# A two-layer encoder trunk in fp32 by three products: up projections and the last down projection with tokens as weights, VectorE squares and transfers within SBUF, attention's result taken from PSUM

## The chip, the cores and the metric

The kernel runs on one core of a Trainium2 chip. The metric is the device time of one execution in microseconds; the time before is 2311.02 us, the median of three runs (2310.91 to 2311.66). The profiled execution took 2311.02 us as well, of which its span in the profile is 2309.3 us; 1.7 us lie around the span.

## The reference, cut to what matters

One sequence of 256 tokens with 2048 features goes through two layers, all in fp32. Layer 0 is attention (16 heads with a relative-position bias over a band of chunks, 16 query heads with a sliding window of two chunks and sinks, rotary), layer 1 a gated linear recurrence. Each is followed by cross-attention into 256 memory tokens (4 heads of 128) and by a gated feed-forward with a causal depthwise convolution over time:

```python
def conv_ffn(h, w_up, conv_w, conv_b, w_down):
    u = causal_depthwise_conv(h @ w_up, conv_w, conv_b)     # h (256, 2048), w_up (2048, 11264), width 3
    val, gate = jnp.split(u, 2, axis=-1)
    return (jax.nn.gelu(gate) * val) @ w_down               # w_down (5632, 2048)
x = x + conv_ffn(rms_norm(x, ffn_norm[layer]), ffn_w_up[layer], ...)
```

The convolution mixes tokens t, t-1 and t-2 of one feature, with weights that belong to the feature.

## The kernel before, in words

**Arithmetic.** Each operand x is split in x_hi (x rounded to fp32r, the type that TensorE multiplies at full rate) and x_lo = x - x_hi, and a product is w_hi x_hi + w_hi x_lo + w_lo x_hi, summed in PSUM. Activations live feature-major: features on the 128 partitions, 256 tokens along the free dimension (`xT`, 16 tiles of 128 features). `xg_hl` and `a_hl` hold the hi and lo halves of a stage's input.

**Units.** All weights come as one stream of 788 units of 128 x 1024 fp32 (512 KB), through four slots. SP loads unit c into `raw` (line 466) once VectorE has split the unit four before it (`lo_done`). ScalarE rounds it to `w_hi` (`split_hi`, line 320) once TensorE has finished the unit four before it (`pe_unit`). VectorE forms `w_lo` (`split_lo`, line 326). TensorE multiplies. The order on every engine is written out by hand as a program per engine; semaphore counts tie the programs together, so an instruction that waits holds everything behind it on its engine.

**Two forms of a unit.** `pair_unit` (lines 342 to 363) has the weights stationary and the tokens moving: 4 feature tiles x 2 output tiles x (one matmul of 512 columns, w_hi against hi and lo side by side, and one of 256 columns, w_lo against hi). The result stands feature-major in two banks, in two halves (main and cross part), which VectorE adds later. `token_unit` (lines 379 to 400) has the tokens stationary and the weights moving: 2 feature tiles x 2 token tiles x three matmuls of 512 columns; the result stands token-major in two banks. Before the change, the attention's input projection and the projections of the memory use the token form, the other large products the pair form; cross-attention has its own two (lines 338 and 374).

**Stages.** In order: `tok` (input projection), `mem` (memory projections, between the attention's groups), `out0`, `xq0`, `xo0` (cross-attention), `up0`, `down0`, `rec`, `out1`, `xq1`, `xo1`, `up1`, `down1`. An up stage has 176 units: the first 8 are woven between units of the cross-attention's output (`WOVEN`), the rest is a loop of 11 iterations of 16 units, one iteration giving 4 value tiles and 4 gate tiles. A down stage has 88 units.

**The feed-forward before.** When a block of 4 units is complete, ScalarE copies its cross part (line 1210), VectorE adds main and cross part into `u_buf` (line 1694) and multiplies by the norm factor per token (line 1653), which TensorE has broadcast over the partitions once per stage (`bcast_pe`, line 439). Then ScalarE makes the tap of the present token with the bias (line 1173), VectorE adds the two earlier tokens' taps (lines 1660, 1665), ScalarE does the GELU (line 1157), VectorE the product (line 1680), ScalarE its rounding (line 1168), VectorE the rest (line 1684). `UP_STEPS` says in which slot of the 16 each step stands.

**Attention before.** Eight groups of four heads. Per group: scores on TensorE (lines 627, 633), softmax on VectorE and ScalarE, 12 transposes (line 650), a copy of these to SBUF, two banks by ScalarE (line 1015) and one by VectorE (line 1454), values (line 665), copy to `oT` (line 1472). Memory units lie between. After the last group ScalarE rounds `oT` (line 1046) and VectorE forms the rest (line 1478), and `out0` starts as the tiles come.

**The end before.** `down1` adds each block to `xT` in two VectorE steps (lines 1537, 1538) and SP writes each pair of tiles (line 507).

Of the kernel before, what the change touches and what calls it, by code (L numbers as in the profile page):

```python
# [16 lines left out]
P = 128  # L17
D_MODEL, SEQ, N_MEM = 2048, 256, 256
KT = D_MODEL // P
# [14 lines left out]
NEG = -1e30  # L34

# [14 lines left out]
WOVEN = [("x", 0), ("x", 1), ("x", 2), ("x", 3), ("x", 4), ("u", 0), ("x", 5), ("x", 6), ("u", 4), ("x", 7), ("u", 1), ("u", 5),  # L50
         ("u", 2), ("u", 6), ("u", 3), ("u", 7)]
UP_STEPS = {0: {8: "g0", 11: "v0", 14: "g1"},
            1: {2: "last", 5: "g0", 8: "v0", 11: "g1", 15: "v1"},
            None: {3: "g0", 7: "v0", 11: "g1", 15: "v1"}}
# [5 lines left out]
UP_BANK = (4, 6, 0, 2)  # L60
# [28 lines left out]
def trunk(nc, t):  # L89
# [3 lines left out]
    with ctx:  # L93
# [19 lines left out]

        xT = sb("xT", [KT, SEQ])
# [8 lines left out]
        a_hi, a_lo = a_hl[:, :, 0, :], a_hl[:, :, 1, :]  # L123
        R1 = AR + size([KT, 2, SEQ])
        R2 = R1 + size([FT - KT, SEQ])
        FFN = top[0]
        u_buf = sb("u_buf", [4, SEQ + 2])
        y_buf = sb("y_buf", [4, SEQ])
        kmem = [at("kmem0", FFN, [XA_HEADS, N_MEM]), sb("kmem1", [XA_HEADS, N_MEM])]
        vmem = [at("vmem0", FFN + 4096, [TT, XA_W]), sb("vmem1", [TT, XA_W])]  # L130
        kmem_tok = [at("kmem_tok0", FFN, [TT, XA_W]), at("kmem_tok1", FFN + size([4, SEQ + 2]) + size([4, SEQ]), [TT, XA_W])]
# [35 lines left out]
        oT = at("oT", O0, [KT, SEQ])  # L167
# [11 lines left out]
        bias_at = [at("bias0", FFN + size([4, SEQ + 2]) + size([4, SEQ]), [3 * COLS]), at("bias1", XG + 12288 + 6144, [3 * COLS])]  # L179
# [10 lines left out]
        x_sq = {name: y_buf if name == "down0" else at(f"x_sq_{name}", R2 + 20480, [4, SEQ])  # L190
# [12 lines left out]
        gate_w = at("gate_w", R2 + 12288, [2, 4, P])  # L203
        cross = at("cross", AR + size([FT - 1, 2, SEQ]), [2, SEQ])
# [27 lines left out]
        pT_ps, pT_act, pT_dve, o_ps, o_done = sem("pT_ps"), sem("pT_act"), sem("pT_dve"), sem("o_ps"), sem("o_done")  # L232
        oT_hi, oT_lo = sem("oT_hi"), sem("oT_lo")
# [7 lines left out]
        tap_done, conv_done, gelu_done = sem("tap_done"), sem("conv_done"), sem("gelu_done")  # L241
# [9 lines left out]
        sp_exp, sp_done = sem("sp_exp"), sem("sp_done")  # L251
        out_done = sem("out_done")
# [15 lines left out]
        for name, k in (("out0", N_BLOCKS), ("xo0", N_BLOCKS), ("up0", FT), ("down0", N_BLOCKS), ("rec", 16), ("out1", N_BLOCKS),  # L268
                        ("xo1", N_BLOCKS), ("up1", FT), ("down1", N_BLOCKS)):
            fblock[name] = n  # L270
            n += k

        cblock = {"up0": 0, "rec": FT, "up1": FT + 16}
# [105 lines left out]
        def token_unit(pe, c, k0, nk, hi, lo, bank, start, stop, ready=None):  # L379

            s, n = c % SLOTS, UE // nk
            if c == 0:
                pe.wait_ge(hi_half, 1)
            else:
                pe.wait_ge(hi_done, c + 1)
            for k in range(nk):
# [4 lines left out]
                for tt in range(TT):  # L391
                    for q, a in enumerate((hi, lo)):
                        nc.tensor.matmul(ps[:, bank + tt, 0:n], a[:, k0 + k, tt * P:tt * P + P], w_hi[:, s, k * n:k * n + n],  # L393
                                         start=start and k == 0 and q == 0, stop=False)
            pe.wait_ge(lo_done, c + 1)
# [6 lines left out]


# [17 lines left out]
        BC = [FFN0, REC, FFN1]  # L421
# [14 lines left out]
        def bcast_pe(pe, n):  # L436
            pe.wait_ge(rb_ready, BC.index(n) + 1)
            for tt in range(TT):
                last = nc.tensor.matmul(ps[:, 2 if n in (FFN0, FFN1) else 6, tt * P:(tt + 1) * P], rb[:, tt, :], ident[:, :],
                                        start=True, stop=True)  # L440
            last.then_inc(rbc_ps, 1)

        def bcast_act(act, n):
            act.wait_ge(rbc_ps, BC.index(n) + 1)
            nc.scalar.activation(r_bc[:, :], ps[:, 2 if n in (FFN0, FFN1) else 6, 0:SEQ], ACT.Copy).then_inc(rbc_ready, 1)

        def sum_squares(pool, src, tiles):

            ch = chains["pool"]
            for tile in tiles:  # L450
# [7 lines left out]
                  (mask[:, :], "mask"), (sinks[:, :, :], "sinks"), (rconst[:, :, :], "rconst"), (fconv[:, :], "fconv0")]  # L458

# [4 lines left out]
        def _(sp):  # L464
# [34 lines left out]
            with sp.Fori(4, N_UNITS // SLOTS) as i:  # L499
                for s in range(SLOTS):  # L500

                    sp.wait_ge(lo_done, i * SLOTS + (s + 1 - SLOTS))
                    unit(s, i * SLOTS + s)
            for b in range(N_BLOCKS):

                sp.wait_ge(proj_free, fblock["down1"] + b + 3)
                sp.dma_start(t["out_t"][:, 2 * b:2 * b + 2, :], xT[:, 2 * b:2 * b + 2, :]).then_inc(out_done, 16)
            sp.wait_ge(out_done, 16 * N_BLOCKS)
# [11 lines left out]
        def pair_tiles(buf, first_tile, n, i=None, per=0):  # L520

            if i is None:
                return buf[:, first_tile:first_tile + n, :]
            return buf[:, bass.ds(i * per + first_tile, n), :]

        def column(buf, index, i=None, per=0):

            return buf[:, index:index + 1] if i is None else buf[:, bass.ds(i * per + index, 1)]
# [5 lines left out]
        SQ_BEFORE = {"out0": 0, "xo0": N_BLOCKS, "down0": 2 * N_BLOCKS, "out1": 3 * N_BLOCKS, "xo1": 4 * N_BLOCKS}  # L534

        AFTER = {"out0": XA0, "xo0": FFN0, "down0": REC, "out1": XA1, "xo1": FFN1, "down1": None}
        UNITS = {"out0": U_BLOCK, "out1": U_BLOCK, "xo0": U_XA_OUT, "xo1": U_XA_OUT, "down0": U_DOWN, "down1": U_DOWN}

        UP_DVE, GATES_AT = 12, 4
        LAST_STEPS = {0: (8,), 1: (9, 10), 2: (11,), 3: (12,), 4: (13,)}  # L540

        def block_done(name, b0, pos):
# [4 lines left out]
            return pos // UNITS[name] if pos % UNITS[name] == UNITS[name] - 1 else None  # L547

# [6 lines left out]
        def _(pe):  # L555
# [42 lines left out]
            def mem_unit(f):  # L598
# [5 lines left out]
                elif u == 0:  # L604

                    pe.wait_ge(mem_free, b)
# [1429 lines left out]
```

## Time and profile before

| | |
|---|---|
| runs | 2311.66, 2311.02, 2310.91 us |
| profiled execution | 2311.02 us, span 2309.3 us, granted clock 1.00 |
| busy | TensorE 2299.1 us (100%), VectorE 1574.2 (68%), ScalarE 1256.0 (54%), GpSimd 189.8 (8%) |
| DMA | 426.94 MB, 185 GB/s on average |

A row of the view of groups gives line, engine, operation, output<-inputs, shapes and count, then the busy time, the mean of one in ns, and the idle time before it with what ended it. A row of the timeline gives start, length, engine, line, operation and count; matmuls are pipelined, so the time of a group of them is read from start to start.

### The profile page before, as it was taken

To read this page: it belongs to the slowest core of one execution; us is meant where nothing else is said; L and a number is where in the kernel's file an instruction comes from. 1 tells how busy PE (TensorE), PEld (TensorE's weight loads), DVE (VectorE), ACT (ScalarE), POOL (GpSimd) and SP (SyncE) were. 2 spreads that over 40 slices of the span, in tenths; PEclk is the share of its full clock that TensorE was granted. 3 is DMA by queue.
4 is the path that set the end of the run, shared out by engine and by line. 5 is a ranking of instruction groups with operands and counts; after the bars stand their busy time and mean duration, and the time that the engine had idled before them with its cause. 6 is when DMAs were issued, how large, how long until landed. Compare 5 with 4: busy or idle time off the path is not lost.

```text
span 2309.3 us, 38203 instructions
## 1 busy us (share of the span) xinstructions
PE 2299.1 (100%) x13184; PEld 2005.1 (87%) x13184; DVE 1574.2 (68%) x1963; ACT 1256.0 (54%) x1701; POOL 189.8 (8%) x171
## 2 busy tenths in 40 slices
PE   9999999999999999999999999999999999999999
PEld 7888888998888888888888888898888888888888
DVE  6776776577777777755555778668777777774443
ACT  6645564466555555544444776556555555553332
POOL 1710002130000000000000100222000000000000
PEclk9999999999999999999999999999999999999999
DMA  8656335445555555555555555535555555555554
GB/s 278 206 189 205 134 117 182 164 164 185 179 200 188 185 190 184 196 190 189 191 187 188 178 184 185 197 133 195 185 191 187 178 200 189 184 190 191 191 187 158
DMA packets 118942, 426.94 MB, mean 185 GB/s; under 512 B 13600, under 2 KB 14496, under 8 KB 118864
## 3 DMA queue, kind: packets, MB, share of 16 engines
q1 hardware_dynamic: 116928, 418.31, 52.9%
q0 software_dynamic: 1792, 7.52, 0.9%
q8 instruction: 51, 0.84, 0.2%
q14 instruction: 27, 0.22, 0.0%
q10 hardware_dynamic: 144, 0.06, 0.0%
HBM read 423.73 MB, written 2.10 MB: 184 GB/s over the span
## 4 chain that ended last, share of the span: by engine, by line
PE 98%; DVE 1%; ACT 1%; issue 0%; DMA 0%; SPq 0%; ACTq 0%; DVEq 0%
PE ps L353 53%; PE ps L357 26%; PE ps L393 8%; PE ps L398 4%; PE ps L338 2%; PE ps L374 2%; PE ps L665 1%; PE ps L852 1%; PE ps L650 0%; PE ps L735 0%; PE ps L572 0%; PE ps L756 0%; DMA xT<-in_x_t 0%; PE ps L633 0%; PE ps L627 0%
## 5 line engine op out<-in xcount | busy, mean ns | idle before, releaser
L326 DVE TENSOR_TENSOR w_lo<-raw,w_hi 128x1024 fp32r<-128x1024 f32 x788 | 970.2, 1237 | 539.5 <-ACT w_hi L320 537.0
L320 ACT ACTIVATE w_hi<-raw 128x1024 fp32r<-128x1024 f32 x787 | 827.3, 1056 | 635.9 <-PE ps L357 499.8
L353 PE MATMUL ps<-xg_hl,w_hi 128*128 128x512 f32 x3328 | 1046.4, 396 | 0.0
L357 PEld LDWEIGHTS ps<-xg_hl,w_lo 128*128 128x128 f32 x3328 | 625.2, 188 | 147.8
L357 PE MATMUL ps<-xg_hl,w_lo 128*128 128x256 f32 x3328 | 653.8, 278 | 0.0
L353 PE MATMUL ps<-a_hl,w_hi 128*128 128x512 f32 x1920 | 603.1, 395 | 0.6 <-DVE a_hl L1478 0.6
L353 PEld LDWEIGHTS ps<-xg_hl,w_hi 128*128 128x128 f32 x3328 | 506.9, 189 | 0.2
L357 PEld LDWEIGHTS ps<-a_hl,w_lo 128*128 128x128 f32 x1920 | 360.7, 188 | 85.2
L357 PE MATMUL ps<-a_hl,w_lo 128*128 128x256 f32 x1920 | 377.2, 278 | 0.0
L353 PEld LDWEIGHTS ps<-a_hl,w_hi 128*128 128x128 f32 x1920 | 292.3, 189 | 0.7 <-DVE w_lo L326 0.7
L1210 ACT ACTIVATE cross<-ps 128x512 f32<-128x512 f32 x104 | 62.0, 596 | 144.5 <-PE ps L357 144.5
L393 PE MATMUL ps<-w_hi,xg_hl 128*128 128x512 f32 (+1 forms) x576 | 136.2, 379 | 1.2 <-DVE xg_hl L1295 1.2
L1173 ACT ACTIVATE y_buf<-u_buf,fconv 128x256 f32<-128x256 f32 x176 | 96.2, 594 | 53.2 <-DVE u_buf L1653 53.2
L393 PEld LDWEIGHTS ps<-w_hi,xg_hl 128*128 128x128 f32 x576 | 103.2, 188 | 21.4 <-DVE xg_hl L1295 1.1
L1694 DVE TENSOR_TENSOR u_buf<-cross,ps 128x512 f32<-128x512 f32 x84 | 57.7, 687 | 89.3 <-ACT cross L1210 89.3
L1660 DVE SCALAR_TENSOR_TENSOR y_buf<-u_buf,fconv,y_buf 128x256 f32<-128x256 f32 x176 | 77.9, 479 | 0.0
L1665 DVE SCALAR_TENSOR_TENSOR y_buf<-u_buf,fconv,y_buf 128x256 f32<-128x256 f32 x176 | 76.9, 478 | 0.1
L398 PE MATMUL ps<-w_lo,xg_hl 128*128 128x512 f32 (+1 forms) x288 | 73.1, 378 | 0.0
L1168 ACT ACTIVATE a_hl<-y_buf 128x512 f32 (+1 forms) x44 | 27.8, 632 | 79.5 <-DVE y_buf L1680 79.5
L393 PE MATMUL ps<-w_hi,a_hl 128*128 128x512 f32 x256 | 66.0, 400 | 0.9 <-ACT kmem_tok L982 0.6
L1653 DVE TENSOR_TENSOR u_buf<-u_buf,r_bc 128x512 f32<-128x512 f32 x88 | 60.8, 691 | 2.6
L398 PEld LDWEIGHTS ps<-w_lo,xg_hl 128*128 128x128 f32 x288 | 52.1, 188 | 10.4 <-DVE w_lo L326 0.4
(198 smaller groups left out, 1486.4 us busy)
## 6 DMA issues: line engine op xcount, KB each, us to landing
raw<-in_w_stream SPq DMA_DIRECT2D x787, 512.0 KB, 3.3
bias<-in_rel_bias POOLq DMA_DIRECT2D x4, 768.0 KB, 6.3
memT<-in_mem_t POOLq DMA_DIRECT2D x4, 512.0 KB, 6.5
gate_w<-in_gate_w POOLq DMA_DIRECT2D x4, 512.0 KB, 3.7
out_t<-xT SPq DMA_DIRECT2D x8, 256.0 KB, 4.3
xT<-in_x_t SPq DMA_DIRECT2D x2, 512.0 KB, 7.6
xT<-in_x_t SPq DMA_DIRECT2D x3, 256.0 KB, 8.9
raw<-in_w_stream SPq DMA_DIRECT2D x2, 256.0 KB, 4.0
```

Source lines behind the costliest of these rows:

```text
L320: nc.scalar.activation(w_hi[:, s, :], raw[:, s, :], ACT.Copy).then_inc(hi_done, 1)
L326: nc.vector.tensor_tensor(w_lo[:, s, :], raw[:, s, :], w_hi[:, s, :].bitcast(F), ALU.subtract).then_inc(lo_done, 1)
L353: nc.tensor.matmul(ps[:, bank + m, :], w_hi[:, s, w], both, start=start and k == ks[0], stop=False, skip_group_check=True)
L357: last = nc.tensor.matmul(ps[:, bank + m, SEQ:2 * SEQ], w_lo[:, s, w], x[:, xk, 0, :], start=False, stop=stop and k == ks[-1], skip_group_ ...
L393: nc.tensor.matmul(ps[:, bank + tt, 0:n], a[:, k0 + k, tt * P:tt * P + P], w_hi[:, s, k * n:k * n + n], start=start and k == 0 and q == 0, ...
L398: last = nc.tensor.matmul(ps[:, bank + tt, 0:n], hi[:, k0 + k, tt * P:tt * P + P], w_lo[:, s, k * n:k * n + n], start=False, stop=stop and ...
L1173: A(y_buf[:, m, :], u_buf[:, m, 2:2 + SEQ], ACT.Identity, scale=column(fconv, w + 2, i, 32), bias=column(fconv, w + 3, i, 32)).then_inc(ta ...
L1210: A(cross[:, :, :], ps[:, bank:bank + 2, SEQ:2 * SEQ], ACT.Copy).then_inc(cross_ready, 1)
L1653: V.tensor_tensor(part, part, r_bc[:, :].unsqueeze(1).to_broadcast([P, 2, SEQ]), ALU.mult).then_inc(u_scaled, 1)
L1660: middle.append(ch.mark(V.scalar_tensor_tensor(y_buf[:, m, :], u_buf[:, m, 1:1 + SEQ], column(fconv, 4 * (4 * half + m) + 1, i, 32), y_buf ...
L1665: ins = V.scalar_tensor_tensor(y_buf[:, m, :], u_buf[:, m, 0:SEQ], column(fconv, 4 * (4 * half + m), i, 32), y_buf[:, m, :], ALU.mult, ALU ...
L1694: V.tensor_tensor(u_buf[:, tile:tile + 2, 2:2 + SEQ], cross[:, :, :], ps[:, bank:bank + 2, 0:SEQ], ALU.add).then_inc(proj_free, 1)
```

## The change

**Up stages.** The units use the token form: 8 units of 512 columns are half an iteration, first the gate half, then the value half, in banks 4, 5 and 6, 7. ScalarE evacuates both banks into `y_up` with the token's norm factor as scale. The columns are ordered on the host so that VectorE can turn 32x32 squares (`up_turn`, into `z_t`) and SP can move the squares to their partitions with 16 transfers within SBUF (`moves`, into `u_t`): for this, token 2q + t stands at place 128t + q of the norm's output (`by_tile_order`), and a run of 64 tokens of each feature lies in `u_t` behind a halo of four places, of which GpSimd copies the two that are needed. `y_up` lies in the memory of `u_t`, so ScalarE waits for `conv_done` before it evacuates. Taps and convolution run half an iteration behind, in slots 12 and 13 for the gate half and 4 and 5 of the next iteration for the value half; product in slot 6, rounding in 7, rest in 8. The last iteration's value half is done in the first slots of the down stage.

**Last down.** Token form, 4 blocks of 22 units. `xT` is turned and moved to `x_tok` (token-major) by four VectorE turns and 16 transfers in `up1`. SP writes token-major output.

**Attention.** The result goes straight from PSUM to hi and lo; the transposed probabilities are all copied by ScalarE; groups 4 to 7 leave out the first 64 keys for the later 128 queries; memory banks are released one by one.

```diff
-WOVEN = [("x", 0), ("x", 1), ("x", 2), ("x", 3), ("x", 4), ("u", 0), ("x", 5), ("x", 6), ("u", 4), ("x", 7), ("u", 1), ("u", 5),
-         ("u", 2), ("u", 6), ("u", 3), ("u", 7)]
+WOVEN = [("x", 0), ("x", 1), ("x", 2), ("x", 3), ("x", 4), ("u", 0), ("x", 5), ("u", 1), ("x", 6), ("u", 2), ("x", 7), ("u", 3),
+         ("u", 4), ("u", 5), ("u", 6), ("u", 7)]
+        y_up = at("y_up", UT, [TT, COLS])
...
# SP, up stage
+                def moves(i, half, bs):
+                    sp.wait_ge(zt_ready, times(TT * (2 * l * UP_ITER + half + 1), i, 2 * TT))
+                    for b in bs:
+                        for a in range(4):
+                            sp.dma_start(u_t[SQ * b:SQ * b + SQ, a, :, :].rearrange("p k n -> p (k n)"),
+                                         z_t[SQ * a:SQ * a + SQ, b, :, :].rearrange("p k n -> p (k n)")).then_inc(ut_in, 16)
...
+                        if u in (7, 15):
+                            moves(i, u // 8, (0, 1))
+                        if u == 8:
+                            moves(i, 0, (2, 3))
+                        if u == 0 and i is not None:
+                            moves(i, -1, (2, 3))
...
# TensorE, up stage
-                        pair_unit(pe, c0 + u, k, xg_hl, 2 * (q % 2), k == 0, k == KT - 4, i, 4 * U_BLOCK)
+                        for u in range(8):
+                            token_unit(pe, c0 + 8 * half + u, 2 * u, 2, xg_hi, xg_lo, UP_BANK[half], u == 0, u == 7, None, None, i, U_UP)
-                bcast_pe(pe, (FFN0, FFN1)[l])
...
# ScalarE
+            def up_tiles(l, i, half):
+                b = 2 * l * UP_ITER + half
+                act.wait_ge(pe_unit, times(first[f"up{l}"] + 8 * (half + 1), i, U_UP))
+                if i is not None or b:
+                    act.wait_ge(conv_done, times(4 * b, i, 8))
+                for tt in range(TT):
+                    A(y_up[:, tt, :], ps[:, UP_BANK[half] + tt, :], ACT.Copy, scale=r_tok[:, (FFN0, FFN1)[l], tt:tt + 1]).then_inc(up_out, 1)
...
+                    for u in range(8 if i is None else 0, U_UP):
+                        split_hi(act, c0 + u + SLOTS, i, U_UP)
+                        if u < 9 and i is not None:
+                            value_slot(l, i, u)
+                        if u % 8 == 7:
+                            up_tiles(l, i, u // 8)
+                        if u in (12, 13):
+                            taps(l, i, 0, 0, (2 * u - 24, 2 * u - 23))
+                        if u == 14:
+                            gate_gelu(l, i)
...
# VectorE
+            def up_turn(l, i, half):
+                b = 2 * l * UP_ITER + half
+                if i is not None or b:
+                    dve.wait_ge(ut_in, times(MOVES * b, i, 2 * MOVES))
+                for tt in range(TT):
+                    dve.wait_ge(up_out, times(TT * b + tt + 1, i, 2 * TT))
+                    V.transpose(z_t[:, :, :, HALO:RUN].rearrange("p b k (i t) -> p t (b k) i", t=TT)[:, tt, :, :],
+                                y_up[:, tt, :].rearrange("p (c j) -> p c j", j=SQ)).then_inc(zt_ready, 1)
...
+            def value_slot(l, i, u):
+                if u in (4, 5):
+                    conv(l, i, 1, 1, (2 * u - 8, 2 * u - 7))
+                if u == 6:
+                    product(l, i, 1)
+                if u == 8:
+                    value_lo(l, i, 1)
...
# attention: ScalarE and VectorE
-                A(probsT[:, 0:2 * COLS], flat(ps[:, 3:5, :]), ACT.Copy).then_inc(pT_act, 1)
+                A(probsT[:, :], flat(ps[:, 3:6, :]), ACT.Copy).then_inc(pT_act, 1)
+                for e in range(2):
+                    A(out_part(g, e, 0), out_ps(e), ACT.Copy).then_inc(o_hi, 1)
-                    last = V.tensor_copy(flat(oT[part, 2 * g:2 * g + 2, :]), ps[part, 4 + e, :])
+                    last = V.tensor_tensor(out_part(g, e, 1), out_ps(e), out_part(g, e, 0).bitcast(F), ALU.subtract)
...
# last down: TensorE and VectorE
-            out_section("down1", g_lo, 2, FT // 2)
+                    for u in range(TOK_DOWN - (n == 3)):
+                        token_unit(pe, c0 + TOK_DOWN * n + u, 2 * u, 2, a_hi, a_lo, bank, u == 0, u == TOK_DOWN - 1,
+                                   value_there if n == 0 else None)
+                for tt in range(TT):
+                    dve.wait_ge(tile_ps, tt + 1)
+                    x = x_tok[:, 3, tt, :]
+                    V.tensor_tensor(x, x, ps[:, 2 + tt, :], ALU.add).then_inc(tile_done, 1)
```

## Rows read from the trace of the kernel before

**Rows 1.** The page's chain that ended last, by engine, share of the span.

```profile
PE 98%; DVE 1%; ACT 1%; issue 0%; DMA 0%; SPq 0%; ACTq 0%; DVEq 0%
```

**Rows 2.** Stretches: length, busy us (instructions) per engine, granted clock, DMA share, GB/s.

```profile
200.00:345.00 145.00, 142.72 (x768) 119.70 (x767) 112.71 (x159) 85.39 (x198) 6.87 (x12) 1.00 0.41 140
496.00:970.00 474.00, 473.98 (x2725) 413.48 (x2724) 356.24 (x472) 269.27 (x344) 4.43 (x5) 1.00 0.55 188
2047.00:2306.00 259.00, 258.46 (x1485) 225.32 (x1483) 126.64 (x119) 98.93 (x98) 0.00 (x0) 1.00 0.54 185
```

**Rows 3.** Timeline (start us, us) of ScalarE, up loop: GELU rows one iteration apart.

```profile
641.54 0.64 ACT L1157 ACTIVATE y_buf<-y_buf 128x512 f32<-128x512 f32 x1 [0.52 <-DVE y_buf L1665]
...
686.12 0.64 ACT L1157 ACTIVATE y_buf<-y_buf 128x512 f32<-128x512 f32 x1 [0.52 <-DVE y_buf L1665]
```

**Rows 4.** Timeline of TensorE, first projections in token form: unit starts, five units apart.

```profile
155.73 1.98 PE L393 MATMUL ps<-w_hi,xg_hl 128*128 128x512 f32 x8
...
169.33 1.98 PE L393 MATMUL ps<-w_hi,xg_hl 128*128 128x512 f32 x8
```

**Rows 5.** Timeline of TensorE, first down stage: sixteen steps apart.

```profile
1000.06 0.62 PE L353 MATMUL ps<-a_hl,w_hi 128*128 128x512 f32 x2
...
1011.20 0.63 PE L353 MATMUL ps<-a_hl,w_hi 128*128 128x512 f32 x2
```

**Rows 6.** Waits of TensorE: us in total, times, longest us.

```profile
PE ps L665 <- DVE probsT L1454: 0.8, 1, 0.8
PE ps L393 <- ACT kmem_tok L982: 0.6, 2, 0.3
PE ps L353 <- DVE a_hl L1478: 0.6, 1, 0.6
...
PE ps L393 <- ACT vmem L982: 0.3, 1, 0.3
```

**Rows 7.** Timeline of TensorE, attention, scores of one group.

```profile
267.06 1.13 PE L627 MATMUL ps<-bkT,bqT 64*128 64x256 f32 x8
268.04 0.60 PE L633 MATMUL ps<-bkT,bqT 64*128 64x128 f32 x4
```

**Rows 8.** Timeline of TensorE, first up stage, broadcast of the norm factors.

```profile
513.23 0.71 PE L439 MATMUL ps<-ident,rb 128*128 128x128 f32 x4
513.70 0.71 PE L353 MATMUL ps<-xg_hl,w_hi 128*128 128x512 f32 x2
```

**Rows 9.** Groups by line: count | busy us, mean ns of one | idle before.

```profile
L326 DVE TENSOR_TENSOR w_lo<-raw,w_hi 128x1024 fp32r<-128x1024 f32 x788 | 970.2, 1237 | 539.5 <-ACT w_hi L320 537.0
L1694 DVE TENSOR_TENSOR u_buf<-cross,ps 128x512 f32<-128x512 f32 x84 | 57.7, 687 | 89.3 <-ACT cross L1210 89.3
...
L320 ACT ACTIVATE w_hi<-raw 128x1024 fp32r<-128x1024 f32 x787 | 827.3, 1056 | 635.9 <-PE ps L357 499.8
L1210 ACT ACTIVATE cross<-ps 128x512 f32<-128x512 f32 x104 | 62.0, 596 | 144.5 <-PE ps L357 144.5
```

**Rows 10.** Timeline of GpSimd and VectorE, up stage: smallest row, two convolution passes.

```profile
506.97 0.71 POOL L425 TENSOR_TENSOR r_tok<-v_tok,neg_half 128x2 f32<-128x2 f32 x1 [3.80 <-DVE v_tok L418]
...
963.03 0.88 DVE L1660 SCALAR_TENSOR_TENSOR y_buf<-u_buf,fconv,y_buf 128x256 f32<-128x256 f32 x2
```

**Rows 11.** Timeline of SP's queue: first and last of five issues in a row.

```profile
34.50 0.43 SPq L475 DMA_DIRECT2D y_rot<-in_rope_g  x1
...
36.40 0.43 SPq L475 DMA_DIRECT2D fconv<-in_fconv  x1
```

**Rows 12.** The page's DMA issues: count, KB each, us to landing.

```profile
raw<-in_w_stream SPq DMA_DIRECT2D x787, 512.0 KB, 3.3
...
out_t<-xT SPq DMA_DIRECT2D x8, 256.0 KB, 4.3
```

**Rows 13.** Timeline at the end: the second of the last two additions, last output.

```profile
2306.22 0.69 DVE L1538 TENSOR_TENSOR xT<-xT,ps 128x512 f32<-128x512 f32 x1
2306.94 0.33 SPq L507 DMA_DIRECT2D out_t<-xT  x1
```

More of the change, by code:

```diff
@@ L498, in _, with units @@
             tables(TABLES)
[L499 to L508, printed above, removed]
+            def units(c0, c1):
+                with sp.Fori(c0 // SLOTS, c1 // SLOTS) as i:
+                    for s in range(SLOTS):
+                        sp.wait_ge(lo_done, i * SLOTS + (s + 1 - SLOTS))
+                        unit(s, i * SLOTS + s)
@@ L626, in scores @@
                     if tile:
-                        last = nc.tensor.matmul(ps[:, j % 2, col * SEQ:(col + 1) * SEQ], q[part, ft, P:SEQ], k, start=True, stop=True)
+                        near = 0 if g < 4 else CHUNK
+                        last = nc.tensor.matmul(ps[:, j % 2, col * SEQ + near:(col + 1) * SEQ], q[part, ft, P:SEQ], k[:, near:SEQ],
+                                                start=True, stop=True)
                     else:
@@ new lines, in conv @@
+            def conv(l, i, back, half, tiles):
+                b = 2 * (l * UP_ITER - back) + half
+                if tiles[0] == 0:
+                    dve.wait_ge(halo_done, times(b + 1, i, 2))
+                for j, count in ((1, mid_done), (0, conv_done)):
+                    for m in tiles:
+                        dve.wait_ge(tap_done if j else mid_done, times(4 * b + m + 1, i, 8))
+                        y = chunks(y_tile(half, m - 4 * back, i))
+                        V.scalar_tensor_tensor(y, u_t[:, :, m, HALO - 2 + j:RUN - 2 + j], column(fconv, 4 * (4 * (1 - half) + m) - 32 * back + j, i, 32),
+                                               y, ALU.mult, ALU.add).then_inc(count, 1)
@@ L1903, in cross_attention, with halos, halo @@
                     G.tensor_tensor(xs[:, 2, h, :], xs[:, 1, h, :], neg_half[:, 0:TT], ALU.pow).then_inc(xrq_ready, 1)
+            def halos(l):
+                def halo(i, half):
+                    pool.wait_ge(ut_in, times(MOVES * (2 * l * UP_ITER + half + 1), i, 2 * MOVES))
+                    one = ones[:, 0:24].rearrange("p (a k n) -> p a k n", a=3, k=4)
+                    G.tensor_tensor(u_t[:, 1:4, :, HALO - 2:HALO], u_t[:, 0:3, :, RUN - 2:RUN], one, ALU.mult).then_inc(halo_done, 1)
+                with pool.Fori(0, UP_ITER) as i:
+                    for half in range(2):
+                        halo(i, half)
             def gate_load(i):
@@ L1932, in _ @@
             out_section("xo1")
+            halos(1)
 def _stream(inp):
```

503 lines of the change are left out of this document (279 added, 224 removed).

## The prediction

> **What bounds the kernel now.** I read the page first, down to its chain of waits: 98% of the chain that ends last is TensorE [rows 1], so only what shortens TensorE's instruction stream, or one of its few waits, can gain. Next the view by stretches [rows 2]: in the up stage TensorE lacks 0.02 of 474 us of being always busy (the second up stage is alike), in the last down stage 0.5 us at its very end; only the attention stage has 2.3 us of idle time in 145. The granted clock is 1.00 in all of them. In the up stage VectorE works 356 us, ScalarE 269, the DMA engines 55%: cover, not bound. Last the pace, since nothing else counts. One weight tile of 128x1024 is a unit. In feature form (weights stationary) it is 16 matmuls, 8 of 512 columns and 8 of 256. In the up loop an iteration of 16 units takes 686.12 - 641.54 = 44.58 us [rows 3], 2.786 us per unit. In token form (tokens stationary) it is 12 matmuls of 512 columns; in the first projections five such units take 169.33 - 155.73 = 13.60 us [rows 4], 2.720 each. Both stream 6144 columns; the difference is four instructions. That it isn't the loop's edge is seen within the first down stage: 16 steps of four matmuls take 1011.20 - 1000.06 = 11.14 us [rows 5], 2.785 per unit, with no edge between.
>
> **The change part by part.**
>
> *Matmul form.* All 2 x 176 up units (8 of each layer are woven into the cross-attention output) and the 88 of the last down go from 16 to 12 matmuls. 440 x (2.786 - 2.720) = 29.0 us. Rows 4 are straight-line code while the up stages loop; since the edge of the old loop cost at most 44.58 - 16 x 2.785 = 0.02 us, I keep it, and let the term go from 25 to 31.
>
> Here a rule of the Trainium skill speaks against the change. Its page "TensorE: Matmul & The Clock Gate" gives the gap of back-to-back matmuls as N/2.4 ns plus about 2.5 ns. By it four fewer save 10 ns a unit, an estimate of 4.4 us in all. The rows have 66 ns a unit, 16 ns for each matmul dropped, and the trace does not agree with so small an overhead. I take the rows.
>
> *Attention.* ScalarE now takes the rounded half of its result from PSUM and VectorE the rest, with no copy that is split once all groups are done. At the start of the output projection TensorE waited 0.6 us for that (a_hl, line 1478); the first unit now needs only groups long done, the last group is asked for in the fourth. ScalarE copies all of the transposed probabilities, so the 0.8 us for VectorE's part (line 1454) goes; ScalarE's copy grows by a half and stays beside the 2.7 us unit that follows the transposes. Each memory bank is released by itself: the 0.6 and 0.3 us for kmem_tok and vmem go [rows 6]. Groups 4 to 7 score 192 keys, not 256: 8 records per group at (268.04 - 267.06)/8 = 0.122 us [rows 7], of which a quarter of the streaming goes, 64/2.4 = 27 ns; x 32 = 0.9 us. Together 3.2. What is late next is the next group's probabilities, two units or more ahead. Bounds 1 to 3.5.
>
> *Norm factors.* The factor per token becomes the scale of ScalarE's evacuation, so the broadcast over partitions goes in both up stages: on TensorE 513.70 - 513.23 = 0.47 us each [rows 8], 0.9 in all. VectorE loses four scalings and four sums of halves per iteration, 0.69 us each.
>
> *The new road of an up tile.* Per half iteration (8 units, 512 columns): ScalarE evacuates two banks (2 x 0.60), VectorE turns 2 x 128x512 in squares, SP issues 16 transfers of 32 rows x 1088 bytes, GpSimd fills the halos; then taps, convolution and product as before, in slots 4 to 8 and 12, 13. TensorE itself waits for banks freed eight units ago and for weights split three units ahead, so all this is hidden while it keeps pace.
> A turn is not in the trace. Below, it could cost ScalarE's 0.60 for 128x512; above, at half the rate, the 1.23 of a pass of 1024 columns [rows 9]. I take the 0.69 of VectorE's own pass of that shape. VectorE then has 16 x 1.23 + 16 x 0.44 + 2 x 1.23 + 4 x 0.69 = 32 of 43.5 us per iteration; ScalarE, 269/474 of it now [rows 2], does about as much as before.
> The page "VectorE: DVE Perf Modes" of the Trainium skill, section "The three transpose paths", gives 311 ns for 128x128 bf16 in 32x32 squares; four of those would be an estimate of 1.24 us, at my upper end, and no row here shows a turn.
> SP issues any size 0.475 us apart (four intervals, 34.50 to 36.40) [rows 11]: 16 moves + 8 loads are 11.4 of 21.8 us. The loads behind the moves go out up to 4 us late. A load is due some 3 units, 8 us, after its slot is free and lands in 3.3 [rows 12]: just covered, and its split is again 3 units ahead of TensorE. The moves add 0.56 MB to each 4.2 MB; 55% becomes 65 to 70%.
>
> *The circle.* The evacuated tile lies where the turned one does, so ScalarE first waits for the convolution of the half before: a chain that closes once per half. From the last landing, value half: halo 0.7 (GpSimd's 0.71), four passes of convolution 1.76 (0.88 for two) [rows 10], split 1.23, 1.76, split 1.23, product 1.23, rounding 1.05, evacuation 1.20, last turn 0.69: 10.9; 16 intervals of SP 7.6; landing 2.4 (the last output, issued 2306.94, ends the span of 2309.3 [rows 13]) to 3.3. Value 20.9 to 21.8. Gate: GELU 1.2 and a split on ScalarE 1.05 in place of split, product and rounding: 19.6 to 20.5. Both halves 40.5 to 42.3 us, TensorE's 16 units 43.5. It fits by 1.2 to 3.0, so I cost it at nothing; if longer, each microsecond costs 22 (11 iterations, 2 layers).
>
> *First down stage, an added wait.* The last value tiles are now finished in its first block, the rest in slot 8. VectorE has five splits, eight convolution passes, product and rest in slots 4 to 8, 12.2 us of 13.9, after a split that can't begin before the ninth unit's end: 1.05 + 1.23 + 1.23 = 3.5, with hand-overs 3.7 us behind it, where the eleventh unit asks 2.8 behind it. 0.9 us of wait; behind it on TensorE stands everything. Bounds 0 to 3. In the last down a block is 22 units, and the tiles are in time.
>
> *Residual in token form.* Four turns and 16 transfers of 128 KB in the last up stage, once; within the same cover. 0, bounds 0 to 4. At the end one addition is left after the last matmul where two stood, the second from 2306.22 [rows 13]: 0.7 us.
>
> *Sum.* 29.0 + 3.2 + 0.9 + 0.7 - 0.9 = 32.9 us. The profiled run's own time is 2311.02 us (span 2309.3, 1.7 around it), and the median of the runs is the same. 2311.0 - 32.9 = 2278.
>
> **The rivals.**
> *A: the circle is longer than 43.5 us.* For it: 1.2 to 3.0 us of slack, and neither a turn nor a transfer within SBUF has a row. With turns at 1.23 a half grows by 1.2 (two in a row), the iteration to 42.9 to 44.7; with landings of 4.3, as the outputs' [rows 12], to 44.3. One of the two costs up to 1.2 x 22 = 26 us: 2290 to 2304. Both make 40.5 + 2.4 + 3.8 = 46.7 us: 3.2 x 22 = 70, so 2348, slower than before. It turns at 43.5 + 32.9/22 = 45.0 us per iteration. Its place: ScalarE's evacuation waits for the convolution, the splits behind it are late, TensorE waits for w_lo. Against both: a move is a fifteenth of a load.
> *B: the form gives next to nothing.* By the rule of the skill's page 4.4 us of the main term are left, then 4.4 + 3.9 = 8 us and 2303. As a mechanism of this kernel it would mean that token units pay elsewhere in a loop what they save, 2.77 us each. Rows 5 speak against it.
> *C: late loads.* If the burst of 16 moves holds a load past its cover, TensorE waits in each half: 44 x 0.3 = 13 us, 2291. For it 11.4 us of issues in 21.8; against it 3 units of cover twice over.
>
> **How the numbers follow.** Forecast 0.75, A with one value bad 0.07, A with both 0.08, B 0.03, C 0.07. Predicted 2278 us. The range of 8 in 10 takes in the bounds of the terms (25 to 31, 1 to 3.5, waits up to 7), C and most of A's first case: 2272 to 2300. A measurement here tells 0.2%, 4.6 us, from no change. Faster 0.88, same 0.03, slower 0.09.
>
> **What would show it.** GELU rows 43.5 us apart in the up loops and TensorE without idle there: the main term. Turn rows near 0.69, moves landing in 2.4 to 3.3 us, an evacuation that waits for TensorE and not for VectorE: the circle. An idle of 1 us before the eleventh unit of the first down stage, none at the start of the attention's output. I am wrong if GELU rows stand more than 43.7 us apart.

## The result, and the profile after

| | us | lowest to highest |
|---|---|---|
| before, 4 runs | 2310.97 | 2310.86 to 2311.66 |
| after, 4 runs | 2366.76 | 2364.79 to 2370.56 |

The changed kernel is slower: ratio 1.0243, 95% interval 1.0231 to 1.0255, that is 55.8 us more where 33 less were forecast. The profiled execution took 2364.79 us, its span is 2363.0 us and its granted clock 0.996.

The page's chain and issues after, answering to [rows 1, 12]. An issue row gives count, KB each and the median us from issue to landing:

```profile
PE 58%; SPq 16%; DMA 8%; issue 6%; DVE 5%; ACT 5%; ACTq 1%; DVEq 0%
PE ps L408 18%; PE ps L366 16%; SPq L539 15%; PE ps L413 9%; PE ps L370 8%; DMA raw<-in_w_stream 8%; PE ps L351 2%; PE ps L387 2%; DVE y_iter L1785 2%; ACT w_hi L333 2%; ACT y_up L1287 1%; DVE z_t L1772 1%; ACT y_iter L1295 1%; SPq L491 1%; DVE w_lo L339 1%
...
raw<-in_w_stream SPq DMA_DIRECT2D x787, 512.0 KB, 3.5
u_t<-z_t SPq DMA_DIRECT2D x704, 34.0 KB, 1.9
```

TensorE had 98% of the chain and has 58%. SP's queue, at 0% before, has 16%, nearly all of it in line 539, the issue of the transfers within SBUF. Note that the transfers themselves (DMA u_t<-z_t) are not among the listed lines at all: it is the issuing that lies on the chain.

The stretches after (us, then busy us and instructions of TensorE, weight loads, VectorE, ScalarE, GpSimd, then clock, DMA share, GB/s), answering to [rows 2]:

```profile
500.00:1008.00 508.00, 482.63 (x2096) 391.06 (x2096) 324.97 (x407) 265.75 (x324) 9.22 (x25) 1.00 0.61 202
1600.00:2120.00 520.00, 493.17 (x2151) 399.41 (x2150) 336.61 (x421) 271.07 (x333) 15.66 (x29) 1.00 0.62 204
2120.00:2359.00 239.00, 235.69 (x1034) 194.62 (x1033) 115.65 (x107) 94.54 (x94) 0.24 (x1) 0.99 0.58 193
```

Both up stages lose: 25.4 and 26.8 us of idle TensorE, at full clock. No other engine is full and the DMA engines are at 61%. Idle time isn't all of the loss: for the same 11416 matmuls TensorE is busy 2291.7 us here and 2268.3 us in e1 below, a kernel that doesn't lose, so some 23 us lie in longer busy rows (the ends of matmuls are modelled). The pace shows both parts. ScalarE's GELU rows, one iteration apart, answering to [rows 3]:

```profile
722.80 1.06 ACT L1301 ACTIVATE y_iter<-y_iter  x1 [1.04 <-DVE y_iter L1785]
769.75 1.06 ACT L1301 ACTIVATE y_iter<-y_iter  x1 [1.04 <-DVE y_iter L1785]
...
958.92 1.06 ACT L1301 ACTIVATE y_iter<-y_iter  x1 [1.04 <-DVE y_iter L1785]
```

From 722.80 to 958.92 there are five iterations, 47.2 us each. Ten iterations take 471.9 us in the first up stage (534.30 to 1006.21) and 476.3 in the second, where the first of the ten takes 50.3 and the others 47.3. The form alone would give 435 for ten. So an iteration is 3.9 us too long on average, and 22 x 3.9 = 86 us is nearly all that separates the result from the forecast (2366.8 - 2278 = 89). SP's queue over one iteration, answering to [rows 11] (a row: start, length of the run of issues, count):

```profile
704.61 4.95 SPq L539 DMA_DIRECT2D u_t<-z_t  x8
709.76 0.43 SPq L491 DMA_DIRECT2D raw<-in_w_stream  x1
710.23 4.94 SPq L539 DMA_DIRECT2D u_t<-z_t  x8
715.37 11.21 SPq L491 DMA_DIRECT2D raw<-in_w_stream  x7
727.32 4.96 SPq L539 DMA_DIRECT2D u_t<-z_t  x8
...
751.51 4.95 SPq L539 DMA_DIRECT2D u_t<-z_t  x8
```

Eight issues take 4.95 us, 0.63 from one to the next with the last issue's own 0.5 at the end. The sixteen of a half, with the one load between them, hold SP from 704.61 to 715.2, where the prediction had 7.6 us. From the first of a half to the first of the next it is 22.7 us (727.32 - 704.61) for the gate half and 24.2 (751.51 - 727.32) for the value half; TensorE's eight units would take 21.8.

### The profile page after: what moved, and what is told of

The parts are those of the page before. It is cut to its first block, busy times and chain, and to the rows that moved or that the text cites. A ratio compares the mean times of both kernels' runs of the same rounds, so it can differ in the third digit from the quotient of the medians.

```text
span 2363.0 us, 34265 instructions
## 1 busy us (share of the span) xinstructions
PE 2291.7 (97%) x11416; PEld 1925.3 (81%) x11416; DVE 1494.1 (63%) x1808; ACT 1253.1 (53%) x1663; POOL 203.4 (9%) x215
## 4 chain that ended last, share of the span: by engine, by line
PE 58%; SPq 16%; DMA 8%; issue 6%; DVE 5%; ACT 5%; ACTq 1%; DVEq 0%
PE ps L408 18%; PE ps L366 16%; SPq L539 15%; PE ps L413 9%; PE ps L370 8%; DMA raw<-in_w_stream 8%; PE ps L351 2%; PE ps L387 2%; DVE y_iter L1785 2%; ACT w_hi L333 2%; ACT y_up L1287 1%; DVE z_t L1772 1%; ACT y_iter L1295 1%; SPq L491 1%; DVE w_lo L339 1%
## 5 line engine op out<-in xcount | busy, mean ns | idle before, releaser
L408 PE MATMUL ps<-w_hi,xg_hl 128*128 128x512 f32 (+1 forms) x3392 | 841.1, 390 | 51.7 <-ACT w_hi L333 48.7
L408 PEld LDWEIGHTS ps<-w_hi,xg_hl 128*128 128x128 f32 x3392 | 627.5, 188 | 200.8 <-ACT w_hi L333 71.3
L413 PE MATMUL ps<-w_lo,xg_hl 128*128 128x512 f32 (+1 forms) x1696 | 450.0, 387 | 0.0
L413 PEld LDWEIGHTS ps<-w_lo,xg_hl 128*128 128x128 f32 x1696 | 316.9, 188 | 66.1 <-DVE w_lo L339 0.4
L366 PE MATMUL ps<-a_hl,w_hi 128*128 128x512 f32 x960 | 304.5, 399 | 8.7 <-DVE a_hl L1797 5.2
L370 PE MATMUL ps<-a_hl,w_lo 128*128 128x256 f32 x960 | 190.0, 280 | 0.0
L366 PE MATMUL ps<-xg_hl,w_hi 128*128 128x512 f32 x512 | 161.7, 397 | 0.0
L370 PEld LDWEIGHTS ps<-xg_hl,w_lo 128*128 128x128 f32 x512 | 96.2, 188 | 22.7
L370 PE MATMUL ps<-xg_hl,w_lo 128*128 128x256 f32 x512 | 100.6, 278 | 0.0
L366 PEld LDWEIGHTS ps<-xg_hl,w_hi 128*128 128x128 f32 x512 | 78.3, 189 | 0.2
```

The source lines that it names most:

```text
L366: nc.tensor.matmul(ps[:, bank + m, :], w_hi[:, s, w], both, start=start and k == ks[0], stop=False, skip_group_check=True)
L370: last = nc.tensor.matmul(ps[:, bank + m, SEQ:2 * SEQ], w_lo[:, s, w], x[:, xk, 0, :], start=False, stop=stop and k == ks[-1], skip_group_ ...
L413: last = nc.tensor.matmul(ps[:, bank + tt, 0:n], hi[:, k0 + k, tt * P:tt * P + P], w_lo[:, s, k * n:k * n + n], start=False, stop=stop and ...
```

## The experiments

Ten kernels ran: e3 and e5 once, e8 ten times, the others four times, beside the kernel before (2311.01 us with e1 to e4, 2310.91 with e5 to e8, 2310.87 with e9 and e10). `u_t`, `z_t`, `moves` are as in the change. In the edits `...` marks what is cut; the counts that the other engines wait for (`MOVES`) follow the number of transfers and aren't shown.

**e1: four transfers per half, each over 128 partitions.**

```diff
-                        for a in range(4):
-                            sp.dma_start(u_t[SQ * b:SQ * b + SQ, a, :, :]..., z_t[SQ * a:SQ * a + SQ, b, :, :]...)
+                        sp.dma_start(u_t[:, b, :, :]..., z_t[:, b, :, :]...)
```

> Changed kernel with 4 transfers of 128 rows per half iteration in place of 16 of 32 rows: same bytes, same waits, same places in the queue, but the squares are not exchanged between partitions (that part of the result is left out). Theory S (the 16 issues of SP, 0.62 us each, make the circle evacuation - turn - moves - taps - convolution longer than TensorE's 8 units, and hold the weight loads behind them): 12 issues fewer take 7.4 us out of each half, the circle falls from 23.7 to some 16 us, TensorE bounds again, GELU rows 43.5 to 43.7 us apart, time 2276 to 2286 us. Rival R (the length comes from the engines' order: convolution, product, evacuation and turn in a row, or from the landing, however many issues): GELU rows stay above 46 us, time above 2345 us.

Measured 2278.48 us (2278.06 to 2279.08), ratio 0.9859 (0.9841 to 0.9876). Its GELU rows in the timeline:

```profile
704.36 1.06 ACT L1300 ACTIVATE y_iter<-y_iter  x1 [0.27 <-DVE y_iter L1784]
...
747.88 1.06 ACT L1300 ACTIVATE y_iter<-y_iter  x1 [0.26 <-DVE y_iter L1784]
```

43.52 us apart, with the same bytes, turns, evacuations, taps and waits. The loss goes with the number of transfers, and not with their landing, which is longer here (3.3 us at the median for 1.9). The two in each burst take 1.12 us, so an issue of 136 KB costs what one of 34 KB costs. Whether it is the issuing or the number of transfers at the DMA engines, e5 tells.

**e2: the sixteen spread over four slots, a load after each four.**

```diff
-                        if u in (7, 15):
-                            moves(i, u // 8, (0, 1))
...
+                        if u in (7, 8, 9, 10):
+                            moves(i, 0, (u - 7,))
```

> Changed kernel with the 16 moves of a half issued four at a time behind four successive weight loads, not eight and eight. It tells apart two ways in which the burst can hurt. If it is the held loads (only one of them goes out in 11 us), they are now late by 2.5 us at most and the time falls to 2280 to 2330 us. If it is the circle alone, the last move goes out no earlier than before (the same 16 issues and two loads more before it), the taps start as late or later, and the time stays at 2365 us or rises to 2400. Theory S holds both, and I expect a part of each: 2320 to 2370.

Measured 2378.26 us (2377.68 to 2382.34), ratio 1.0295 (1.0276 to 1.0313): slower than the changed kernel and above the 2320 to 2370 that I expected; the result lies where the text has "the circle alone". No load is held by more than four transfers any more (2.4 us), but the last transfer goes out 1.1 us later in its half, after three loads, and what stands in the chain now is the transfer's own road:

```profile
PE ps L408 17%; PE ps L366 16%; SPq L539 13%; PE ps L413 9%; PE ps L370 8%; DMA u_t<-z_t 4%; ACT w_hi L333 3%; DVE y_iter L1785 2%; SPq L491 2%; PE ps L351 2%; PE ps L387 2%; ACT y_iter L1295 2%; ACT y_up L1287 2%; DMA raw<-in_w_stream 1%; DVE z_t L1772 1%
```

DMA raw<-in_w_stream fell from 8% to 1%, DMA u_t<-z_t came with 4%. I read this as two roads from one half's issues to the next half's, one by the load behind them and one by their landing, and both hold all sixteen.

**e3: 24 issues per half, the same bytes.** Transfers of a = 0 and 1 are cut in two.

```diff
...
+                            for k0, k1 in ((0, 2), (2, 4)) if a < 2 else ((0, 4),):
+                                sp.dma_start(u_t[SQ * b:SQ * b + SQ, a, k0:k1, :]..., z_t[SQ * a:SQ * a + SQ, b, k0:k1, :]...)
```

> Changed kernel with 24 issues per half in place of 16 (two of four transfers per group cut in two), same bytes. Theory S: 8 more issues of 0.62 us lengthen each of 44 halves by 5.0 us, 218 us in all: 2585 us, 2550 to 2620; GELU rows 57 us apart. Rival R: 2365 to 2390 us.

Measured 2587.77 us, in one run. SP's queue:

```profile
715.71 7.48 SPq L540 DMA_DIRECT2D u_t<-z_t  x12
723.83 0.34 SPq L491 DMA_DIRECT2D raw<-in_w_stream  x1
724.29 7.50 SPq L540 DMA_DIRECT2D u_t<-z_t  x12
```

Twelve in 7.48 us are 0.63 apart again (four more than eight in 2.53 us more), though eight of them are of 17 KB and only four of 34. GELU rows at 711.20 and 768.74 are 57.5 us apart: some 10.2 us more than after for 16 more issues, 0.64 each. Past the point from which it decides, every issue is on the path with its full length. TensorE's granted clock was 0.92 in e3's first up stage, where it waits more than in any other run; the issues alone account for the time (44 x 8 x 0.63 = 222 us, measured 221.0), so it cost nothing that can be seen.

**e4: the exchange through HBM.** One write of the turned half to a scratch in HBM, then four reads, each into 32 partitions with four runs of 1088 bytes; the result is the same.

```diff
+                    if bs[0] == 0:
+                        sp.wait_ge(zt_ready, ...)
+                        sp.dma_start(t["scratch"][half % 2].rearrange("b a j m -> (a j) b m"), z_t[:, :, :, :]...).then_inc(z_out, 16)
+                        return
+                    sp.wait_ge(z_out, ...)
+                    for b in range(4):
+                        sp.dma_start(u_t[SQ * b:SQ * b + SQ, :, :, :]..., t["scratch"][half % 2][b].rearrange("a j m -> j a m")).then_inc(ut_in, 16)
```

> Changed kernel, same result, with the exchange of squares made by one write of 128 rows to HBM and four reads of 32 rows x 4 runs of 1088 bytes per half: 5 issues in place of 16, one more landing (some 2.4 us) in the road, 1.1 MB of HBM traffic more per half. Theory S: issues cost 3 us in place of 10.6, the second landing adds 2.4 and the wait for its slot on SP 1 to 3: the circle comes to 18 to 21 us, below TensorE's 21.8, and the time to 2278 to 2295 us, faster than both kernels. Rival R: the added landing makes it slower than the changed kernel, above 2370 us.

Measured 2279.45 us (2278.89 to 2280.55), ratio 0.9862 (0.9844 to 0.988). It beats both kernels with the same result. SP's queue and the issues:

```profile
711.17 0.38 SPq L539 DMA_DIRECT2D scratch<-z_t  x1
712.83 0.33 SPq L492 DMA_DIRECT2D raw<-in_w_stream  x1
716.74 1.76 SPq L544 DMA_DIRECT2D u_t<-scratch  x4
...
scratch<-z_t SPq DMA_DIRECT2D x44, 544.0 KB, 4.7
u_t<-scratch SPq DMA_DIRECT2D x176, 136.0 KB, 2.9
```

The road now has two landings, 4.7 + 2.9 = 7.6 us, and moves twice the bytes (the DMA engines are busy at 76% of the up stage, 61% after). Yet from the first issue to the last landing it is about 10.2 us (711.17 to 718.5 + 2.9), where sixteen issues and a landing took 12.5. GELU rows stand 43.5 apart. These reads, from HBM, are issued 0.45 apart; so the rate of [rows 11] holds for them and not for transfers within SBUF. What it is in a transfer within SBUF that makes its issue dearer, no run shows.

**e5: half of the transfers issued by GpSimd.**

```diff
# GpSimd
+                    pool.wait_ge(zt_ready, ...)
...
+                    for b in (2, 3):
+                        for a in range(4):
+                            pool.dma_start(u_t[SQ * b:SQ * b + SQ, a, :, :]..., z_t[SQ * a:SQ * a + SQ, b, :, :]...).then_inc(ut_in2, 16)
```

> Changed kernel, same result, with 8 of the 16 moves of a half issued by GpSimd, at once when the turns are done, and 8 by SP as before. Theory S (the number of issues in one queue, on the circle): SP's burst falls from 10.6 to 5.0 us; GpSimd needs some 1 us for an issue, 8 us beside it. The circle falls by 2 to 5 us per half, below or just at TensorE's pace: 2280 to 2320 us. If what hurts is the transfers themselves (their count on the DMA engines), nothing changes: 2360 to 2375 us.

Measured 2286.34 us in one run, 24.6 us under the kernel before beside it. The two queues work at once:

```profile
709.33 4.96 SPq L540 DMA_DIRECT2D u_t<-z_t  x8
709.52 3.98 POOL L2051 DMA_DIRECT2D u_t<-z_t  x8
```

All sixteen are out in 5 us in place of 10.6, and GELU rows stand 43.5 apart. In the loop the same sixteen transfers on two queues cost nothing: it is neither their number at the DMA engines nor their landing (2.4 and 2.2 us here, 1.9 after). GpSimd's issues are 0.50 us apart, half of what I had supposed. Of the 7.9 us by which e5 stands above e1, 7.7 lie in the second up stage (ten iterations 441.8 us, in e1 434.1), at its start, in and behind the iteration in which SP also issues the residual's 16 transfers.

**e6: twelve issues per half**, of 64, 32 and 32 partitions. As in e1, the squares are not exchanged.

```diff
+                        for r0, r1 in ((0, 64), (64, 96), (96, 128)):
+                            sp.dma_start(u_t[r0:r1, b, :, :]..., z_t[r0:r1, b, :, :]...)
```

> Changed kernel with 12 transfers per half (per group one of 64 rows and two of 32), same bytes; the squares are not exchanged (that part of the result is left out). From 24 issues (iteration 57.4 us) and 16 (47.3) the circle costs 1.25 us of iteration per issue, so 12 issues make 42.3 us, under TensorE's 43.5: the time is that of 4 issues, 2277 to 2284 us. If instead something else of the 16 moves costs (a queue that fills, held loads), 12 issues lie between, 2300 to 2345 us.

Measured 2279.81 us (2278.53 to 2280.31), ratio 0.9862 (0.9846 to 0.9879); SP's six in a row take 3.68 us. Twelve fit. With the 0.63 per issue of e3, the 3.9 us by which sixteen miss are some six issues an iteration, three a half: by this estimate the point from which it decides is at 13; between 12 and 16 nothing was run.

**e7: the evacuated tile in memory of its own in the second up stage.** ScalarE then needn't wait for the convolution there.

```diff
-                    act.wait_ge(conv_done, times(4 * b, i, 8))
+                    if l:
+                        act.wait_ge(zt_ready, times(TT * b, i, 2 * TT))
+                    else:
+                        act.wait_ge(conv_done, times(4 * b, i, 8))
-                    A(y_up[:, tt, :], ...
+                    A(y_up[l][:, tt, :], ...
```

> Changed kernel, same result, in whose second up stage the evacuated tile has its own memory, so ScalarE's evacuation no longer waits for the convolution but for the turn before. My prediction put the place of the circle at this wait. If that is right, the second up stage runs at TensorE's pace: 2367 - 42 = 2325 us. If the circle is closed by the order of ScalarE's program (taps of the moved tile stand before the next evacuation, GELU and product wait for the convolution anyway), nothing changes: 2362 to 2370 us, GELU rows of the second up stage 47.3 us apart. I expect the second.

Measured 2366.04 us (2364.5 to 2367.18), ratio 1.0232 (1.0215 to 1.025), and the second up stage's GELU rows 47.4 apart in the loop, 47.3 after: no change. The wait that the prediction named isn't what closes the circle. Behind the transfers, ScalarE's program itself has taps, splits and the GELU ahead of the evacuation, and the GELU waits for the convolution anyway.

**e8: e4 with sixteen matmuls per unit.** The same columns stream, the w_lo part cut in eight of 256.

```diff
-                    last = nc.tensor.matmul(ps[:, bank + tt, 0:n], ...)
+                    for h in range(2):
+                        last = nc.tensor.matmul(ps[:, bank + tt, h * 256:h * 256 + 256], ...)
```

> e4_by_hbm, same result, in which each unit of the up stages and the last down does its w_lo part in 8 matmuls of 256 columns in place of 4 of 512: 16 matmuls and 6144 columns as in the feature form. If the gain of the token form is the number of matmuls, it goes: 439 x 66 ns = 29 us, 2308 us (2303 to 2312). If only the isolated gap of some 2.5 ns per matmul counts, 4 us: 2284 us.

Measured 2310.89 us (2309.64 to 2312.61), 31.4 us above e4. One unit on TensorE in e8, then in e4, timeline of the first up stage:

```profile
699.76 2.00 PE L409 MATMUL ps<-w_hi,xg_hl 128*128 128x512 f32 x8
701.61 1.11 PE L417 MATMUL ps<-w_lo,xg_hl 128*128 128x256 f32 x8
702.56 2.00 PE L409 MATMUL ps<-w_hi,xg_hl 128*128 128x512 f32 x8
```

```profile
701.97 1.98 PE L409 MATMUL ps<-w_hi,xg_hl 128*128 128x512 f32 x8
703.78 1.07 PE L414 MATMUL ps<-w_lo,xg_hl 128*128 128x512 f32 x4
704.69 1.98 PE L409 MATMUL ps<-w_hi,xg_hl 128*128 128x512 f32 x8
```

2.80 against 2.72 us. 31.4 us over some 439 units are 72 ns a unit, 18 ns for each matmul, with nothing else changed. It is the main term of the forecast, taken back by itself.

**e9 and e10: evacuation, turn, taps and convolution ahead of the split of their slot**, on ScalarE and VectorE; e9 with the transfers as after, e10 as in e2.

```diff
+                        if u % 8 == 7:
+                            up_tiles(l, i, u // 8)
+                        if u in (4, 5) and i is not None:
+                            taps(l, i, 1, 1, (2 * u - 8, 2 * u - 7))
+                        if u in (12, 13):
+                            taps(l, i, 0, 0, (2 * u - 24, 2 * u - 23))
                         split_hi(act, c0 + u + SLOTS, i, U_UP)
...
```

> Sixteen transfers as in the changed kernel, but in the up loops ScalarE does its evacuation (slots 7, 15) and its taps (slots 4, 5, 12, 13) ahead of the split of that slot, and VectorE its turn and its convolution likewise; the rounding of the value half comes behind the evacuation. First theory (the circle closes through the loads that go out behind the 16 transfers: the split waits for its load, and evacuation and taps stand behind the split): the loop through the load, the split and TensorE's last two units stays, 10.76 + 3.4 + 1.06 + 5.44 + 2.0 = 22.7 us in the gate half, and the value half falls from 24.2 to about that, so an iteration takes 45.4 to 46.3 us in place of 47.3 and the kernel 2336 us (2322 to 2352). Second theory (the convolution and the evacuation close the circle wherever the splits stand): 2360 to 2368. Third (without this order TensorE keeps pace in spite of 16 issues): 2280 to 2290.

> The same order as in the run before, with the transfers spread over four slots with a load between them, so that no load is held by more than four transfers. First theory (the loads' road is open here and what is left is the road of the transfers themselves: 16 issues and 3 loads 12.0, landing 2.0 to 2.5, taps, convolution, evacuation and turn): the gate half falls from 23.2 by up to two splits of ScalarE to 21.8 to 22.5, the value half from 25.1 by 0.5 to 2, the iteration from 48.4 to 45.5 to 47.5 us, and the kernel to 2335 us (2314 to 2358). Second theory (order of the engines is nothing to it): 2378.

e9 took 2354.03 us (2352.33 to 2355.48), 12.7 less than after but above its range; its iteration is 46.9 us. e10 took 2413.45 (2411.09 to 2414.9), 35 more than e2: a clear miss. Why, the timelines show. In e9, around a turn:

```profile
743.50 1.30 DVE L1774 STREAM_TRANSPOSE z_t<-y_up 128x512 f32<-128x512 f32 x2
...
744.73 2.31 DVE L339 TENSOR_TENSOR w_lo<-raw,w_hi 128x1024 fp32r<-128x1024 f32 x2
...
746.52 1.78 SPq L539 DMA_DIRECT2D u_t<-z_t  x3
```

The turn ends at 744.80, but the first transfer goes out at 746.52, 1.7 us later, not 0.1: SP has the load of that slot ahead of the transfers, that load waits for the split, and the split now stands behind the turn. In e10, taps moved forward wait for the landing with the splits behind them:

```profile
726.39 1.09 ACT L1295 ACTIVATE y_iter<-u_t,fconv 128x256 f32 x2 [9.09 <-DMA u_t<-z_t]
```

Nine us of waiting for the landing, 2.5 at most after, with the next splits behind it. TensorE's granted clock was 0.96 in e10's first up stage and 0.99 in e2's; how much of the 35 us that is, was not taken apart. So little is left of my first theory of e9: the loads' road shrinks as it said (DMA raw<-in_w_stream has 1% of e9's chain, 8% after), but the value half, which it had fall to 22.7 us, still takes 24.3 (722.22 to 746.52), and the edits made two new waits of their own. Neither order brings sixteen issues under 43.5 us.

## Why the prediction was wrong

**The step that failed** is the circle, costed at nothing because it fitted by 1.2 to 3.0 us, and in it the term "16 intervals of SP 7.6", worked out from "SP issues any size 0.475 us apart". [Rows 11] show loads from HBM. Issues within SBUF are 0.63 apart, from 17 KB to 136 KB, and the prediction left out the load that stands between the two bursts of a half: together the term is 10.6 us. Put into the prediction's circle of 40.5 to 42.3 us, 3.0 us more in each half give 46.5 to 48.3; measured 47.2 in the first up stage and 47.6 in the second. That this comes so close is in part luck: the landing was shorter than forecast by 0.5 to 1.4 us a half, and the circle doesn't close where the prediction had it. The price of a microsecond held: 22 x 3.9 = 86 us. "Size" was read into five rows that vary in size but not in where the data come from and go, and the bounds were set for the turn and the landing, the two things without a row, while the term that came sixteen times over was given none. The prediction's own sign of being wrong, GELU rows more than 43.7 us apart, is what came.

**Rival A** was the right kind of thing (the circle longer than 43.5 us; the page's chain shows it), with a wrong cause. The two values that it doubted both came out good: the landing took 1.9 us (2.4 to 3.3 forecast) and the turn 0.69, as forecast:

```profile
701.61 1.06 ACT L1305 ACTIVATE a_hl<-y_iter  x1 [1.47 <-DVE y_iter L1793]
702.57 1.25 ACT L1287 ACTIVATE y_up<-ps,r_tok 128x512 f32<-128x512 f32 x2
703.27 1.31 DVE L1772 STREAM_TRANSPOSE z_t<-y_up 128x512 f32<-128x512 f32 x2 [0.66 <-ACT y_up L1287]
704.61 4.95 SPq L539 DMA_DIRECT2D u_t<-z_t  x8
```

Two turns take 1.31 us for 128x512 fp32. The estimate of 1.24 each from the bf16 figure in "VectorE: DVE Perf Modes" of the Trainium skill, section "The three transpose paths", doesn't hold here. The place was wrong as well. The prediction had the evacuation wait for the convolution, and e7 takes that wait away for nothing. The chain of after runs, in the gate half, from the last transfer's issue (715.2) to the load issued behind it (715.37, landed 3.4 us later) and to ScalarE's split of that load at 718.76. Behind that split ScalarE's program has the second taps, the GELU, which waits for their convolution, and another split, and only then the evacuation (724.72), the turn and the next first issue (727.32). In the value half it runs from the sixteenth issue through the load at 738.6 (3.5 us), the split, then taps, convolution, product, rounding. A load waited for behind a burst, that split, and what TensorE waits for:

```profile
713.88 1.06 ACT L333 ACTIVATE w_hi<-raw 128x1024 fp32r<-128x1024 f32 x1 [5.80 <-DMA raw<-in_w_stream]
...
718.76 1.06 ACT L333 ACTIVATE w_hi<-raw 128x1024 fp32r<-128x1024 f32 x1 [0.99 <-PE ps L413]
...
719.87 2.11 PE L408 MATMUL ps<-w_hi,xg_hl 128*128 128x512 f32 x8 [1.16 <-ACT w_hi L333]
```

The first of them waits for the one load between the bursts (709.76). The second is put down to TensorE by the profile, but the unit that it needs finished, four before its own, had ended at 710.6; what came last was the load. Over the whole run, in the view of TensorE's waits (us in total, times, longest us):

```profile
PE ps L408 <- ACT w_hi L333: 53.1, 38, 3.3
PE ps L366 <- DVE a_hl L1797: 5.2, 1, 5.2
```

So TensorE waits 38 times for the rounded weights (w_hi), and not for w_lo as the prediction had it.

**Rival C** (a load held past its cover, priced at 13 us) named this wait, but as an accident of 0.3 us per half; the 38 waits are of 1.4 us on average. It is one of two roads of the same circle: e2 all but takes it out of the chain and meets the other.

**Rival B** is out. The form alone is worth 31.4 us in e8's reverse edit, 18 ns for each matmul. By the 2.5 ns that the Trainium skill, page "TensorE: Matmul & The Clock Gate", section "Back-to-back issue gap", gives for the isolated gap of a matmul, it would be 4.4 us (an estimate), and the measurement decides.

**The other terms**, read where the circle is open (e1 and e4). *Form*: GELU rows 43.52 apart for 44.58 [rows 3], 66 ns a unit, as forecast. *Residual in token form*: nothing in e1, as forecast; in after itself the iteration of the second up stage with its 16 transfers takes 50.3 us where the others take 47.3. *Sum*: 2278.5 and 2279.5 for 2278. *Norm factors*: the broadcast is gone from TensorE. *First down*: one wait of TensorE, as forecast 0.9 us, in e4's view of waits:

```profile
PE ps L367 <- DVE a_hl L1802: 0.9, 1, 0.9
...
PE ps L776 <- DVE kmem_tok L1555: 0.3, 1, 0.3
PE ps L409 <- ACT vmem L1118: 0.2, 1, 0.2
PE ps L409 <- ACT kmem_tok L1118: 0.2, 1, 0.2
```

*Attention*, read in after: from the first scores to the output projection 136.8 us for 139.4, a gain of 2.6 where 3.2 were forecast. The waits for the probabilities and for the output are gone; those for the memory banks shrank to 0.2 each and did not go, and a new one of 0.3 came (kmem_tok, line 1555 of e4) [rows 6]. *Narrower scores*, after, answering to [rows 7]:

```profile
268.23 0.92 PE L721 MATMUL ps<-bkT,bqT 64*128 64x192 f32 x8
```

The matmuls behind these start at 268.99, 0.76 us later for 0.98: 0.22 x 4 = 0.9, as forecast. *The end*: one addition of 0.69 us is left after the last matmul, as forecast. The first scores come 1.3 us later in after (204.32 for 202.98) and 1.5 in e4, but 0.4 earlier in e1 and 0.7 in e8, with the same program up to there: it differs from one execution to the next and isn't the change's.

In after itself the last value tiles come late as well: TensorE waits 5.2 us for them once (a_hl, line 1797, in the rows above) where e1 and e4 wait 0.9, the circle's last turn. With the 86 us of the loops this makes up about the whole distance from the forecast.

## What to carry to other kernels

A count of small instructions is a term with a price per instruction, and the price has to come from a row of the same kind: same queue, same memory at both ends. When a step closes a loop between queues, add every instruction issued on it, compare with the pace it must keep, and give the widest bounds to what is multiplied most. When many small transfers within SBUF are on such a loop, fewer and larger ones can win even by a detour: five issues through HBM with two landings beat sixteen with one by 87 us. And before moving a step ahead of a split, follow what the other queues wait for behind that split: both of my reorderings made a wait of their own.

## What the runs showed of the hardware

- Issue on SP's queue: 0.63 us from one to the next within SBUF (8 in 4.95, 12 in 7.48, of 17 and 34 KB; 6 in 3.68 with two of 68 KB in e6), 0.45 for reads of 136 KB from HBM into SBUF (4 in 1.76).
- Issue on GpSimd's queue within SBUF: 0.50 us (8 in 3.98), beside SP's eight, which stayed at 4.96 (one run).
- Landing within SBUF: 1.9 us for 34 KB over 32 partitions, 3.3 for 136 KB over 128 (e1); through HBM 4.7 for the write of 544 KB and 2.9 for a read of 136 KB.
- A turn of 128x512 fp32 in 32x32 squares on VectorE: 0.69 us at the median of 88.
- Splitting four matmuls of 512 columns into eight of 256, each with its weight load, costs 18 ns for each one added.
